# One ring of eight PSUM banks, and transposes of the new inverse instead of a second product in each level of the delta rule

## The chip, the cores and the metric

The kernel runs on one core of a Trainium2 chip. The metric is the device time of one execution in microseconds (us), as the median of several runs. TensorE (PE), VectorE (DVE), ScalarE (ACT), GpSimd (POOL) and SyncE (SP, which issues the DMAs) each run their own list of instructions and wait for one another on semaphores.

## The reference

One sequence of 512 tokens of width 1024, in fp32, goes through two blocks. The change touches the gated delta rule of the first block: 8 heads, keys and values of width 128, in chunks of 64 tokens. Cut to its core:

```python
h = rms_norm(x, norm1_w) * (1 + scale1) + shift1
proj = h @ w_in                                       # q, k, v, z, alpha, beta, attention, gates
qkv = silu(causal_dwconv(concat(dn_q, dn_k, dn_v), dn_conv_w))      # 4 taps over time
q, k = l2_norm(...), l2_norm(...)                     # per head
decay = exp(gc[:, None] - gc[None, :]) on the lower triangle       # gc = cumsum(g)
a_mat = strict_lower((k * beta) @ k.T * decay)        # 64 x 64 for each chunk and head
u, w = triangular_solve(I + a_mat, [v * beta, k * beta * exp(gc)])
intra = lower((q @ k.T) * decay)
# then the recurrence over 8 chunks: v_new = u - w S;  o = q_e S + intra v_new;  S = dec S + k_dec.T v_new
```

The rest of the first block is latent attention, output projections, a gated mix and a feed-forward part with a convolution. The second block has spatial gating, gated linear attention, band attention, a convolution of 31 taps, a gated merge and a feed-forward part.

## The kernel before

One function, `program(f)`, lists the stages; it is run once for each engine's class (`Tensor`, `Scalar`, `Vector`, `Gpsimd`), whose methods issue what that engine does. So the order of the calls is the order of each engine's queue. Stages that share time are generators, and `weave(main, side, n_main, n_side)` (L179) steps them: after each step of `main` it takes n_side / n_main steps of `side`. A point such as `dp_ve xt 2 h` is a semaphore value that the producer raises and others wait for.

**Linears.** A step of `main` is one unit: 128 output columns for all 512 tokens, made by 24 matmuls of 128x512 (three fp32r products, high x high, low x high, high x low, for each of 8 slices of the 1024 inputs) into one PSUM bank. The high halves of the weights (`whi`) are split off by ACT (L357), the low halves (`wlo`) by DVE or POOL (L360). A unit named dn0 to dn23 is a head's q, k or v; ACT and DVE then read its bank for the convolution, on DVE three `SCALAR_TENSOR_TENSOR` taps (L368), and ACT applies silu. Between them stand small matmuls of the modulation (`ada`), a few steps after certain units.

**Banks.** PSUM has eight banks, each 128 x 512 fp32. A `Banks` object is a ring: `take` gives the next bank that isn't held, `free` is the point at which the last user of that bank has read it, and PE waits for that point before it writes. `PL` (L332) has banks 0 to 2 for the units, `PA` (L333) has banks 3 to 7 for all other products of the program.

**The delta rule's side work** is `prep(h, w)`, four pairs of heads one after the other, the two heads of a pair stepped in turn. Its products each fill one bank with four 128x128 blocks (two chunks of 64 in each). A head's steps on PE: the sums of squares for k and q (`sq`); the decay row (`g`); `kk` and `qk` and the beta row (`b`); a transpose of k (`kt`); a transpose of the first inverse Xt (`x`); then levels 1 to 5; then `v` (a transpose), `w` and `u`. The stretch from `sq` to the first product of level 1 is called the preamble here, the rest the levels. ACT takes ln and exp of the norms, copies evacuated blocks, and DVE scales k and q, forms the decay differences (L365), and multiplies the masks in.

A level doubles the blocks of which the inverse is known. Xm holds the inverse, Xt its transpose, Bm the part of A of this level (made by POOL, `bm`), Dm the evacuated product. Level lv makes t = Bm' Xm (ACT copies it to Dm), then Xm -= Xt' Dm (`xm`) and Xt -= Dm' Xt (`xt`), the two subtractions on DVE from PSUM. Level 5 updates Xt alone. In the trace a fp32 matmul of 128x128 shows as two rows and a transpose (L345) as one.

**Order.** The units ahead of the stage are the first four of `qkv`; the rest of them, with the small projections behind them, run against the four pairs' side work, 21 rounds to a pair, 3.33 to a unit (30 : 100, the numbers of `weave`). SP's list of weight loads is written by the same stages and follows the buffers.

## Time and profile before

| | |
|---|---|
| median of 3 runs | 2551.38 us (2550.47 to 2552.47) |
| profiled execution | 2550.77 us |
| its span on the core | 2548.8 us |
| PE busy | 2361.8 us (93%), 10928 rows |
| DVE busy | 1090.6 us (43%), 1588 rows |
| ACT busy | 926.9 us (36%), 1352 rows |
| POOL busy | 699.7 us (27%), 415 rows |
| chain that ended last | PE 76%, DVE 11%, ACT 7% |
| mean granted clock of PE | 0.961 |

The span is the profiler's time from the first to the last instruction; the execution's own time is 2.0 us longer. The chain that ended last is followed back from the last instruction, and its shares tell on which engine the end rests. A busy share is the time in which an engine had an instruction in work; matmuls overlap, and the end of each is modelled.

### The profile page before, as it was taken

The page shows a single profiled execution, that of the slowest core. Times are in us where ns is not written, and L with a number is a line of the kernel's source. Part 1 is how long each engine was busy: PE and PEld are TensorE (multiplying, and loading weights), DVE is VectorE, ACT ScalarE, POOL GpSimd, SP SyncE. Part 2 cuts the span into 40 slices and gives each one's busy share as a digit, 9 for nine tenths or more (in the row PEclk, how much of TensorE's full clock was granted, in tenths as well). Part 3 has the DMA queues.
Part 4 walks back from the last instruction along what each step waited for, and adds up shares of the span by engine and source line. Part 5 has one row for each costly group of instructions (what it writes and reads, how often), then busy time and mean ns, then how long its engine had stood idle before and what let it go on. Part 6 is the DMA issues. An engine that isn't in the chain of part 4 may idle for free.

```text
span 2548.8 us, 27018 instructions
## 1 busy us (share of the span) xinstructions
PE 2361.8 (93%) x10928; PEld 1883.4 (74%) x10928; DVE 1090.6 (43%) x1588; ACT 926.9 (36%) x1352; POOL 699.7 (27%) x415
## 2 busy tenths in 40 slices
PE   8798989999899999899999887999999999999996
PEld 4577877986567677688888676787777777888875
DVE  2576656455443432433321599413443242322333
ACT  2544423233433432533322332334552433332334
POOL 1141144001211235222223241321132353332332
PEclk9898989999999899999999898999999999999998
DMA  8222223121122133333333421332221332333341
GB/s 263 75 67 68 73 59 100 50 75 54 38 66 70 42 99 95 117 95 96 95 99 99 124 75 58 92 99 66 83 67 58 108 91 76 107 92 98 100 123 50
DMA packets 347983, 220.65 MB, mean 87 GB/s; under 512 B 18393, under 2 KB 327244, under 8 KB 347860
## 3 DMA queue, kind: packets, MB, share of 16 engines
q1 hardware_dynamic: 338462, 202.31, 27.3%
q10 hardware_dynamic: 9398, 16.62, 2.0%
q8 instruction: 87, 1.43, 0.2%
q14 instruction: 36, 0.29, 0.0%
HBM read 210.49 MB, written 8.41 MB: 86 GB/s over the span
## 4 chain that ended last, share of the span: by engine, by line
PE 76%; DVE 11%; ACT 7%; issue 3%; POOL 2%; DMA 1%; ACTq 0%; SPq 0%; DVEq 0%; POOLq 0%
PE ps L342 74%; DVE arena L368 4%; ACT arena L357 3%; DVE arena L360 2%; DVE scr L368 1%; PE ps L345 1%; POOL wlo L360 1%; ACT whi L357 1%; ACT scr L357 1%; ACT L353 1%; POOL arena L360 1%; DVE wlo L360 1%; DVE arena L365 1%; DVE scr L360 0%; POOL scr L360 0%
## 5 line engine op out<-in xcount | busy, mean ns | idle before, releaser
L342 PE MATMUL ps<-hhi,whi 128*128 128x512 f32 x1664 | 676.6, 407 | 53.3 <-POOL wlo L360 32.3
L360 POOL TENSOR_TENSOR wlo<-wraw,whi 128x1024 fp32r<-128x1024 f32 (+1 forms) x163 | 389.7, 2391 | 1204.7 <-ACT whi L357 1204.7
L342 PE MATMUL ps<-hlo,whi 128*128 128x512 f32 x1664 | 661.5, 398 | 0.0
L342 PE MATMUL ps<-hhi,wlo 128*128 128x512 f32 x1664 | 660.7, 397 | 0.0
L357 ACT ACTIVATE whi<-wraw 128x1024 fp32r<-128x1024 f32 (+1 forms) x328 | 340.7, 1040 | 359.7 <-PE ps L342 298.1
L342 PEld LDWEIGHTS ps<-hhi,whi 128*128 128x128 f32 x1664 | 322.0, 194 | 134.7 <-issue 47.6
L342 PE MATMUL ps<-arena 128*128 128x128 f32 (+6 forms) x2304 | 341.6, 301 | 34.7 <-ACT arena L357 12.9
L360 DVE TENSOR_TENSOR wlo<-wraw,whi 128x1024 fp32r<-128x1024 f32 (+2 forms) x165 | 213.8, 1296 | 369.2 <-ACT whi L357 369.0
L342 PEld LDWEIGHTS ps<-hhi,wlo 128*128 128x128 f32 x1664 | 320.3, 192 | 69.4
L342 PEld LDWEIGHTS ps<-hlo,whi 128*128 128x128 f32 x1664 | 321.3, 193 | 68.0 <-issue 3.2
L342 PEld LDWEIGHTS ps<-arena 128*128 128x128 f32 (+1 forms) x2304 | 286.7, 197 | 70.0 <-issue 28.3
L357 ACT ACTIVATE arena<-ps 128x512 f32<-128x512 f32 (+5 forms) x223 | 116.4, 540 | 332.1 <-PE ps L342 277.1
L342 PE MATMUL ps<-h,whi 128*128 128x512 f32 x512 | 159.9, 394 | 1.1 <-POOL wlo L360 1.1
L357 ACT ACTIVATE scr<-ps,colv 128x512 f32<-128x512 f32 x78 | 55.4, 711 | 246.2 <-PE ps L342 241.1
L368 DVE SCALAR_TENSOR_TENSOR scr<-ps,colv,scr 128x511 f32<-128x511 f32 (+2 forms) x116 | 86.8, 749 | 132.6 <-ACT scr L357 130.2
L368 DVE SCALAR_TENSOR_TENSOR arena<-arena,colv 128x512 f32<-128x512 f32 (+1 forms) x136 | 132.0, 975 | 16.3 <-ACT arena L357 12.6
L360 DVE TENSOR_TENSOR arena<-ps,arena 128x512 f32<-128x512 f32 (+1 forms) x88 | 55.6, 640 | 153.3 <-PE ps L342 151.4
L360 DVE TENSOR_TENSOR scr<-ps,scr 128x512 f32<-128x512 f32 x86 | 59.1, 689 | 138.6 <-PE ps L342 137.0
L360 POOL TENSOR_TENSOR arena<-arena,scr 128x512 f32<-128x512 f32 x57 | 77.8, 1368 | 138.4 <-ACT scr L357 96.8
L342 PEld LDWEIGHTS ps<-h,whi 128*128 128x128 f32 x512 | 97.1, 190 | 22.6 <-issue 2.6
L342 PE MATMUL ps<-ff,whi 128*128 128x512 f32 x352 | 108.4, 389 | 0.0
L360 POOL TENSOR_TENSOR arena<-arena,cst 128x512 f32<-128x512 f32 (+1 forms) x48 | 62.2, 1309 | 144.3 <-PE ps L342 76.7
(190 smaller groups left out, 2691.9 us busy)
## 6 DMA issues: line engine op xcount, KB each, us to landing
wraw<-in_w_in_dram SPq DMA_DIRECT2D x99, 512.0 KB, 3.9
wraw<-in_w_ff_dram SPq DMA_DIRECT2D x64, 512.0 KB, 4.0
wraw<-in_ffn_w_up_dram SPq DMA_DIRECT2D x44, 512.0 KB, 3.9
wraw<-in_w_ada_dram SPq DMA_DIRECT2D x32, 512.0 KB, 3.9
wraw<-in_w_gate_dram SPq DMA_DIRECT2D x32, 512.0 KB, 3.9
arena<-in_w_ada_dram SPq DMA_DIRECT2D x8, 1024.0 KB, 11.5
wraw<-in_ffn_w_down_dram SPq DMA_DIRECT2D x16, 512.0 KB, 3.9
wraw<-in_w_branch_dram SPq DMA_DIRECT2D x16, 512.0 KB, 3.4
```

The lines of the kernel that those rows point to most:

```text
L342: return pe.e.matmul(o, l, r, start=start, stop=stop)
L345: return pe.e.transpose(o, i, CST[0:n, C_ID:C_ID + n])
L353: ac.e.preload_act_table_set("natural_log_exp_and_others")
L357: return ac.e.activation(o, i, f, bias=bias, scale=scale, **kw)
L360: return q.e.tensor_tensor(o, a, b, op)
L365: return q.e.tensor_scalar(o, a, s1, s2, op0, op1)
L368: return ve.e.scalar_tensor_tensor(out=o, in0=a, scalar=s, in1=b, op0=op0, op1=op1)
```

## The change

Three edits. First, the two rings become one of eight banks, for the units and everything else. Second, in levels 1 to 4 the product `xm` and its subtraction on DVE go. In their place PE transposes the updated Xt (`turn_xt`, four transposes into one bank), which waits for DVE's subtraction `xt`, and ACT copies the bank to Xm (`copy_x`); t of the next level waits for that copy. A level then has three steps (t, xt, x) instead of two. Third, the numbers of `weave` go from 30 : 100 to 30 : 120, four side steps to a unit instead of 3.33; the side work of a pair has 25 rounds after and 21 before.

```diff
--- before.py
+++ after.py
@@ -329,8 +329,7 @@
         SG = Signals(lambda name: ctx.enter_context(nc.semaphore(name)), values)
         inc, at, last = SG.inc, SG.at, SG.last
         pe, ve, ac, po, sp = (Engine() for _ in range(5))
-        PL = Banks(SG, PS[0:3], places)
-        PA = Banks(SG, PS[3:8], places)
+        PL = PA = Banks(SG, PS, places)
         SCR = [SCRT[:, i, :] for i in range(NSC)]
         ident = CST[:, C_ID:C_ID + P]
         ones = CST[:, C_ONE:C_ONE + P]
@@ -836,7 +835,7 @@
             for _ in range(4):
                 next(first)
             f.token_cols()
-            weave(chain(first, paced(f.small_proj(), more)), f.prep_pairs(), 30, 100)
+            weave(chain(first, paced(f.small_proj(), more)), f.prep_pairs(), 30, 120)
             f.rec_start()
             weave(paced(f.mla_proj(), more), f.recur(), 8, 16)
             run(more)
@@ -1133,6 +1132,16 @@
                 EG, Dm, Am, Xm, Xt, Bm = (A[:, 36 + 6 * w + i, :] for i in range(6))
                 q, k, v = A[:, QB + h, :], A[:, KB + h, :], A[:, VB + h, :]
                 blk = [slice(b * P, (b + 1) * P) for b in range(4)]
+
+                def turn_xt(lv):
+                    bk = PA.take("dn", h, "x", lv)
+                    pe.wait_ge(*PA.free("dn", h, "x", lv))
+                    pe.wait_ge(*at("dp_ve", "xt", lv, h))
+                    for s in blk:
+                        t = tr(bk[:, s], Xt[:, s])
+                    t.then_inc(*inc("dp_mm", "x", lv, h))
+                    PA.put(("dn", h, "x", lv), "dp_act", "x", lv, h)
+
                 while 16 + h not in self.have:
                     yield
                 yield
@@ -1179,33 +1188,18 @@
                 t.then_inc(*inc("dp_mm", "kt", h))
                 PA.put(("dn", h, "kt"), "dp_ve", "kb", h)
                 yield
-                bk = PA.take("dn", h, "x")
-                pe.wait_ge(*PA.free("dn", h, "x"))
-                pe.wait_ge(*at("dp_ve", "xt", 0, h))
-                for s in blk:
-                    t = tr(bk[:, s], Xt[:, s])
-                t.then_inc(*inc("dp_mm", "x", h))
-                PA.put(("dn", h, "x"), "dp_act", "x", h)
+                turn_xt(0)
                 yield
                 for lv in range(1, 6):
                     bk = PA.take("dn", h, "t", lv)
                     pe.wait_ge(*PA.free("dn", h, "t", lv))
                     pe.wait_ge(*at("dp_po", "bm", lv, h))
-                    pe.wait_ge(*at("dp_act", "x", h) if lv == 1 else at("dp_ve", "xm", lv - 1, h))
+                    pe.wait_ge(*at("dp_act", "x", lv - 1, h))
                     for s in blk:
                         t = mm(bk[:, s], Bm[:, s], Xm[:, s], True, True)
                     t.then_inc(*inc("dp_mm", "t", lv, h))
                     PA.put(("dn", h, "t", lv), "dp_act", "t", lv, h)
                     yield
-                    if lv < 5:
-                        bk = PA.take("dn", h, "xm", lv)
-                        pe.wait_ge(*PA.free("dn", h, "xm", lv))
-                        pe.wait_ge(*at("dp_act", "t", lv, h))
-                        pe.wait_ge(*at("dp_ve", "xt", lv - 1, h))
-                        for s in blk:
-                            t = mm(bk[:, s], Xt[:, s], Dm[:, s], True, True)
-                        t.then_inc(*inc("dp_mm", "xm", lv, h))
-                        PA.put(("dn", h, "xm", lv), "dp_ve", "xm", lv, h)
                     bk = PA.take("dn", h, "xt", lv)
                     pe.wait_ge(*PA.free("dn", h, "xt", lv))
                     pe.wait_ge(*at("dp_act", "t", lv, h))
@@ -1215,6 +1209,9 @@
                     t.then_inc(*inc("dp_mm", "xt", lv, h))
                     PA.put(("dn", h, "xt", lv), "dp_ve", "xt", lv, h)
                     yield
+                    if lv < 5:
+                        turn_xt(lv)
+                        yield
                 bk = PA.take("dn", h, "v")
                 pe.wait_ge(*PA.free("dn", h, "v"))
                 pe.wait_ge(*at("qkv", 16 + h))
@@ -1709,6 +1706,11 @@
             def prep(self, h, w):
                 EG, Dm, Am, Xm, Xt, Bm = (A[:, 36 + 6 * w + i, :] for i in range(6))
                 q, k, v = A[:, QB + h, :], A[:, KB + h, :], A[:, VB + h, :]
+
+                def copy_x(lv):
+                    ac.wait_ge(*at("dp_mm", "x", lv, h))
+                    act(Xm, PA.of("dn", h, "x", lv)[:, :], ACT.Copy).then_inc(*inc("dp_act", "x", lv, h))
+
                 while 16 + h not in self.have:
                     yield
                 if h < 2:
@@ -1736,8 +1738,7 @@
                 yield
                 yield
                 yield
-                ac.wait_ge(*at("dp_mm", "x", h))
-                act(Xm, PA.of("dn", h, "x")[:, :], ACT.Copy).then_inc(*inc("dp_act", "x", h))
+                copy_x(0)
                 yield
                 for lv in range(1, 6):
                     ac.wait_ge(*at("dp_mm", "t", lv, h))
@@ -1745,6 +1746,9 @@
                     act(Dm, PA.of("dn", h, "t", lv)[:, :], ACT.Copy).then_inc(*inc("dp_act", "t", lv, h))
                     yield
                     yield
+                    if lv < 5:
+                        copy_x(lv)
+                        yield
                 yield
                 ac.wait_ge(*at("dp_mm", "w", h))
                 act(k, PA.of("dn", h, "w")[:, :], ACT.Copy).then_inc(*inc("dp_act", "w", h))
@@ -2476,12 +2480,11 @@
                 yield
                 for lv in range(1, 6):
                     yield
-                    if lv < 5:
-                        ve.wait_ge(*at("dp_mm", "xm", lv, h))
-                        tt(ve, Xm, Xm, PA.of("dn", h, "xm", lv)[:, :], ALU.subtract).then_inc(*inc("dp_ve", "xm", lv, h))
                     ve.wait_ge(*at("dp_mm", "xt", lv, h))
                     tt(ve, Xt, Xt, PA.of("dn", h, "xt", lv)[:, :], ALU.subtract).then_inc(*inc("dp_ve", "xt", lv, h))
                     yield
+                    if lv < 5:
+                        yield
                 ve.wait_ge(*at("dp_mm", "v", h))
                 ve.wait_ge(*at("dp_po", "bm", 5, h))
                 tt(ve, b4(Am), b4(PA.of("dn", h, "v")[:, :]), per_tok(TB), ALU.mult).then_inc(*inc("dp_ve", "vb", h))
@@ -3065,6 +3068,8 @@
                         level(lv + 1)
                     yield
                     yield
+                    if lv < 5:
+                        yield
                 yield
                 yield
 
@@ -3325,7 +3330,7 @@
             sp.e, SG.engine = eng, "sp"
             sync_program()
 
-        return SG.points, {**PL.made, **PA.made}
+        return SG.points, PL.made
 
 
 # ---- launch: one core; inputs and outputs as the reference has them ----
```

On TensorE, the levels of the second pair of heads (levels 1 and 2), between the unit dn5 and the next one. `ps3` is bank 3, each row is a head's product or transpose. Before (t and xt, xm of two heads in turn, from the first level's xm on):

```order
L342 MATMUL ps3<-arena 128x128 x4
L342 MATMUL ps4<-arena 128x128 x4
L342 MATMUL ps5<-arena 128x128 x4
L342 MATMUL ps6<-arena 128x128 x4
L342 MATMUL ps7<-arena 128x128 x4
L342 MATMUL ps3<-arena 128x128 x4
L342 MATMUL ps4<-arena 128x128 x4
L342 MATMUL ps5<-arena 128x128 x4
L342 MATMUL ps6<-arena 128x128 x4
L342 MATMUL ps7<-arena 128x128 x4
```

After, at the same place in the program, behind dn5 (t and xt of level 2, then x, then t of level 3):

```order
L341 MATMUL ps7<-arena 128x128 x4
L341 MATMUL ps0<-arena 128x128 x4
L341 MATMUL ps1<-arena 128x128 x4
L341 MATMUL ps2<-arena 128x128 x4
L344 MATMUL ps3<-cst,arena 128x128 x4
L344 MATMUL ps4<-cst,arena 128x128 x4
L341 MATMUL ps5<-arena 128x128 x4
L341 MATMUL ps6<-arena 128x128 x4
```

Ten products became eight rows, of which two are transposes (L344, the old L345); in each level the transposes stand behind the xt that they read, with the other head's xt or x between, and the banks run through all eight.

On TensorE, the preamble of the third pair of heads (4 and 5). `gb,sel` are the decay and beta rows. Before, behind the unit dn22 and ahead of the products of the modulation:

```order
L342 MATMUL ps6<-arena 128x128 x4
L342 MATMUL ps7<-arena 128x128 x4
L342 MATMUL ps3<-gb,sel 128x512
L342 MATMUL ps4<-arena 128x128 x4
L342 MATMUL ps5<-arena 128x128 x4
L342 MATMUL ps6<-gb,sel 128x512
L345 MATMUL ps7<-cst,arena 128x128 x4
L345 MATMUL ps3<-cst,arena 128x128 x4
L345 MATMUL ps4<-cst,arena 128x128 x4
L345 MATMUL ps5<-cst,arena 128x128 x4
```

After, the same products stand ahead of dn22, behind `sq`:

```order
L341 MATMUL ps3<-gb,sel 128x512
L341 MATMUL ps4<-gb,sel 128x512
L341 MATMUL ps5<-arena 128x128 x4
L341 MATMUL ps6<-arena 128x128 x4
L341 MATMUL ps7<-gb,sel 128x512
L341 MATMUL ps0<-arena 128x128 x4
L341 MATMUL ps1<-arena 128x128 x4
L341 MATMUL ps2<-gb,sel 128x512
```

and behind dn22:

```order
L344 MATMUL ps4<-cst,arena 128x128 x4
L344 MATMUL ps5<-cst,arena 128x128 x4
L344 MATMUL ps6<-cst,arena 128x128 x4
L344 MATMUL ps7<-cst,arena 128x128 x4
L341 MATMUL ps0<-arena 128x128 x4
L341 MATMUL ps1<-arena 128x128 x4
L341 MATMUL ps2<-arena 128x128 x4
L341 MATMUL ps3<-arena 128x128 x4
```

kk and qk of both heads moved ahead of dn22; the transposes stay behind it, and now t of level 1 and its xt follow in the same place between the units.

## Rows read from the trace of the kernel before

**Rows 1.** The profile's page: span, and busy us of TensorE and VectorE.

```profile
span 2548.8 us, 27018 instructions
...
PE 2361.8 (93%) x10928; PEld 1883.4 (74%) x10928; DVE 1090.6 (43%) x1588; ACT 926.9 (36%) x1352; POOL 699.7 (27%) x415
```

**Rows 2.** Windows: us, busy us of PE, PEld, DVE, ACT, POOL (rows), PEclk, DMA share, GB/s.

```profile
121.40:467.60 346.20, 315.68 (x1898) 270.94 (x1897) 211.40 (x302) 135.34 (x203) 109.96 (x78) 0.94 0.25 71
```

**Rows 3.** The same view, sum over the four stretches of levels.

```profile
sum 195.10, PE 192.92 PEld 178.14 DVE 116.36 ACT 59.21 POOL 61.79; mean PE 48.23 PEld 44.54 DVE 29.09 ACT 14.80 POOL 15.45
```

**Rows 4.** The same view: preambles of the second, third and fourth pair.

```profile
217.10:247.00 29.90, 21.15 (x85) 15.01 (x84) 21.70 (x36) 13.97 (x20) 7.62 (x8) 0.81 0.22 68
306.80:344.30 37.50, 29.82 (x125) 23.03 (x124) 21.89 (x37) 15.41 (x22) 12.68 (x10) 0.77 0.19 57
398.40:423.50 25.10, 22.69 (x108) 16.56 (x108) 17.70 (x28) 13.77 (x21) 9.98 (x9) 1.00 0.24 70
```

**Rows 5.** TensorE's waits in the stage: us in total, times, longest us.

```profile
PE ps L345 <- DVE arena L360: 9.5, 6, 3.7
PE ps L342 <- DVE arena L365: 8.8, 6, 3.2
```

**Rows 6.** Timeline of TensorE: start us, us, line, op, count [idle before].

```profile
199.95 1.04 PE L345 MATMUL ps<-cst,arena 128*128 128x128 f32 x8
200.82 3.74 PE L342 MATMUL ps<-arena 128*128 128x128 f32 x32
```

**Rows 7.** Timeline of all engines around a unit and a level, second pair.

```profile
249.83 0.48 PE L342 MATMUL ps<-hhi,whi 128*128 128x512 f32 x1
...
255.38 3.73 PE L342 MATMUL ps<-arena 128*128 128x128 f32 x32
255.58 0.69 ACT L357 ACTIVATE scr<-ps,colv 128x512 f32<-128x512 f32 x1 [3.93 <-PE ps L342]
...
256.30 2.32 DVE L368 SCALAR_TENSOR_TENSOR scr<-ps,colv,scr 128x511 f32<-128x511 f32 x3 [3.21 <-ACT scr L357]
258.54 2.47 DVE L360 TENSOR_TENSOR arena<-arena,ps 128x512 f32<-128x512 f32 x4
...
259.36 3.67 PE L342 MATMUL ps<-arena 128*128 128x128 f32 x28 [0.25 <-DVE arena L360]
...
260.53 0.60 ACT L357 ACTIVATE arena<-ps 128x512 f32<-128x512 f32 x1 [3.74 <-PE ps L342]
```

**Rows 8.** Timeline of TensorE in the second pair's preamble.

```profile
226.89 1.16 PE L342 MATMUL ps<-arena 128*128 128x128 f32 x8 [1.95 <-DVE arena L365]
229.20 2.07 PE L342 MATMUL ps<-arena 128*128 128x128 f32 x8 [1.15 <-DVE arena L365]
...
231.93 0.79 PE L342 MATMUL ps<-hhi,whi 128*128 128x512 f32 x1
...
239.23 1.03 PE L345 MATMUL ps<-cst,arena 128*128 128x128 f32 x8
243.94 1.09 PE L345 MATMUL ps<-cst,arena 128*128 128x128 f32 x4 [3.67 <-DVE arena L360]
246.12 1.11 PE L345 MATMUL ps<-cst,arena 128*128 128x128 f32 x4 [1.09 <-DVE arena L360]
```

**Rows 9.** Windows, three microseconds of the unit at 231.93.

```profile
232.50:235.50 3.00, 3.00 (x8) 2.31 (x7) 2.97 (x4) 0.00 (x0) 3.00 (x5) 0.50 0.00 0
```

**Rows 10.** Timeline of TensorE at the start of the program.

```profile
9.79 5.74 PE L345 MATMUL ps<-cst,arena 128*128 128x128 f32 x33 [6.33 <-DMA arena<-in_x_dram]
```

**Rows 11.** Windows, two pieces of that run of transposes.

```profile
9.80:13.70 3.90, 3.90 (x19) 3.90 (x20) 2.30 (x4) 2.82 (x5) 0.00 (x0) 1.00 1.05 388
13.80:15.50 1.70, 1.70 (x17) 1.53 (x16) 1.70 (x4) 0.00 (x0) 0.00 (x0) 1.00 1.05 387
```

**Rows 12.** Timeline of TensorE ahead of the stage.

```profile
82.57 0.80 PE L342 MATMUL ps<-hhi,whi 128*128 128x512 f32 x1 [4.63 <-ACT arena L357]
...
100.78 0.77 PE L342 MATMUL ps<-hhi,whi 128*128 128x512 f32 x1 [5.69 <-POOL wlo L360]
```

## The prediction

> **What bounds the kernel now.** I read the page first. TensorE (PE) works for 2361.8 of 2548.8 us [rows 1], VectorE (DVE) and ScalarE (ACT) for less than half of it. So what counts is work taken from PE, and places where PE stands still. The edits touch one stage, from the first side work of the delta rule to the end of the fourth pair of heads, 346.2 us with 315.68 us of PE work [rows 2]. Windows cut it into two kinds of stretch. In the four stretches of levels (the doubling of the inverse, then v, w, u) PE is busy 192.92 of 195.10 us: a pure PE bound [rows 3]. In the four preambles (norms, kk, qk, decay, transposes, up to the first product of level 1) it stands still for 8.75, 7.7 and 2.4 us in the second, third and fourth (stretch less PE busy), with a granted clock of 0.81, 0.77 and 1.00 [rows 4]. The list of waits of the stage says who is waited for: its two costliest lines name DVE [rows 5]. So there are two prices, work in the levels and stalls in the preambles.
>
> **A. PE work in the levels.** Each head makes `xm` at levels 1 to 4: 8 x 4 = 32 products of four 128x128 matmuls. An fp32 matmul is two rows of the trace. 32 rows from 200.82 on show 3.74 us [rows 6]; some 0.2 us of it is the modelled tail of the last, so 0.112 us a row, and a head's four matmuls take 8 x 0.112 = 0.894 us. A transpose is one row: 8 rows from 199.95 to 200.82, 0.109 us each, and a head's four take 0.437 us [rows 6]. Replaced one for one: 32 x (0.894 - 0.437) = **-14.6 us**, sure at full clock. The 32 DVE subtractions that go (0.6 us each) and the 32 ACT copies that come (0.60 us, the row at 260.53 [rows 7]) move 19 us from one engine to the other; both have room, so neither is counted as such.
>
> **B. Handovers in the levels.** Before, `xm` and `xt` both need only the copy of t, and four products of two heads lie beside the evacuations. After, one level is the chain t, ACT copy, xt, DVE subtraction, transposes, ACT copy, t. PE has two heads to alternate, and now and then a projection unit (24 rows, 5.5 us, 249.83 to 255.38 [rows 7]). By the new order of TensorE I walked the 16 level-and-pair places:
> - No unit between xt and x, nine times. Four rows of the other head's xt (0.894 us) cover part of head 0's evacuation, which needs the product's tail, two semaphore steps and 0.6 us of DVE. What is left I take as 0.6: 5.4 us.
> - A unit with a convolution stands ahead of xt and x directly (in pair 0 and 1, and once in pair 2), three times. DVE must run the three taps first (256.30, 2.32 us, behind ACT's reading of the unit's bank) and subtracts from 258.54 on [rows 7]. The second xt ends by 1.79 us after the unit, x's input is there some 3.98 us after it: 2.2 us of wait, 2.65 with the second head. 8.0 us. Before, the same 3.98 us was covered by four products, leaving the 0.25 us at 259.36 [rows 7].
> - A unit ahead of x and then t, four times: ACT's copy for t stands behind what ACT does with the unit's bank (0.69 us at 255.58 and a second step like it [rows 7]); about 1.1 each, 4.5 us.
> - t to xt, as today, seven times 0.16: 1.1 us.
> Together 19.0 us, less what the same places cost today by starts of rows (0.2 to 0.4 beyond the pace; 259.36 less 255.38 is 3.98 where 32 rows need 3.58 [rows 7], some 13 of them, 5.4 us): **+13.6 us**. Bounds: 0, if the evacuations hide (two heads alternate), and +22, if every x costs like the middle kind for both heads. I take the walk. A and B nearly cancel.
>
> **C. Preambles.** The third edit gives 4 side steps per unit instead of 3.33, and the two orders shift what stands where; the ring changes which bank a product waits for.
> - Pair 1. Today PE stops 1.95 and 1.15 us for a bank that the DVE decay step frees, runs the unit of 231.93 in 7.3 us up to 239.23 against 5.5, and stops 3.67 and 1.09 us for the transposes' input [rows 8]. With the short waits ahead of kk that is 11.6 us. Now one unit stands between the squares and g (it hides the ln, exp and normalising chain) and the waits for banks go: with eight banks the one that kk takes was freed long before. What comes back: head 2's x still needs DVE's chain, and three taps, 2.32 us as at 256.30, stand ahead of it [rows 7]; 3.6 us, and 2 us of lower clock. **-6** (-7.4 to -5).
> - Pair 2. Its stretch is the longest, 37.5 us with 29.82 us of PE work at clock 0.77 [rows 4]: 7.7 us idle, and about 5 us of slow pace. The six products go ahead of a unit now, the transposes follow it, and level 1 starts at once. The ln chain is uncovered, about 4 us as today, and 1.6 us ahead of x: 12.7 - 5.6 = **-7** (-8.6 to -5).
> - Pair 0: two units lie in its chain of ACT and DVE today, one after: **+2.5** (0 to +4). Pair 3: busy 22.69 of 25.10 us at clock 1.00 today [rows 4]; here the unit that hid the ln chain moves behind it: **+1** (0 to +2.5).
> Sum **-9.5 us**, bounds -12 (each at its best) and 0 (the chain of DVE sets each preamble whatever PE does).
>
> **D. The clock in the levels.** Where PE stood still in the preamble the granted clock fell: 0.50 (1.2 GHz) for 232.50 to 235.50, three microseconds of the unit that stands behind two bank waits [rows 8, 9]. Such a fall costs that unit 1.9 us, 7.3 against 5.5 [rows 7, 8]. B puts waits of 2.2 us and less into the levels, with dense work between them; the two waits of pair 1 before the fall were 1.95 and 1.15 within 6 us [rows 8]. I take half a fall: **+1** (0 to +14, seven falls).
> Transposes alone seem to lift the clock: the program's first 33 rows are transposes after 6.33 us of idleness [rows 10], and the window at 9.80 has 19 rows in 3.90 us, the one at 13.80 17 in 1.70 us, 0.205 and 0.100 each [rows 11]. The clock column reads 1.00 in both, but the pace halves within one run of rows, from that of 1.2 GHz to that of 2.4, with no matmul between. The Trainium skill says otherwise (TensorE: Matmul & The Clock Gate, Part 4, PE-mode transpose): a transpose doesn't count as busy for the clock gate. By that sentence the 128 new transposes would be idle time and the fall of D would come in most levels, with the sum some 10 us nearer to no change; by the rows they keep the clock, and the sum stands. The trace disagrees with the page so far as pace tells it, and I go by the trace.
>
> **E. The ring elsewhere.** Outside the stage PE waits for a bank at few places. The longest, 4.63 us at 82.57, stands ahead of a stop of 5.69 us at 100.78 for weights that POOL splits, which takes up what is won [rows 12]; of smaller ones in the second block I take: **-1.5 us** (-4 to 0). If a projection unit met a bank whose reader is late, it would be a loss; with eight in turn each bank was put seven products earlier, and I see none.
>
> **Sum.** -14.6 + 13.6 - 9.5 + 1 - 1.5 = -11.0 us on the profiled execution's 2550.77 us: 2539.8. The median, 2551.38, stands 0.6 us above it: **2540.5 us**. 0.2% (5.1 us) is about what a measurement of this kernel can tell from no change.
>
> **The rivals.**
> - The preambles don't shorten (C = 0). For it: DVE is busy 21.70 of 29.90 us there [rows 4], so its chain may set the end whatever PE does; against: a bank wait is no data, and PE's stops are in both halves. A + B + D + E = -1.5: **2549.9 us**. No measurable change. Chance 0.20.
> - The handovers hide (B at half, +6). For it: PE has only 2.2 us of idleness in the four stretches today, two heads alternate, and ACT is busy for 59.21 of their 195.10 us, so its copy rarely stands in a queue [rows 3]. Then 2540.5 - 7.6 = **2533 us**. Chance 0.15.
> - Slower: the clock. The waits ahead of x and t fall in level after level; if each of the seven places behind a unit ended in a fall, every next unit would run as 231.93 did, with the level's products beside it, 2.4 us a place [rows 8]: +17 in place of D's +1, and the preambles' gain goes with the same falls: about **2557 us**. It decides from about four falls with C at half. Against: the fall in [rows 9] stands behind two waits close together with little between them, and B's have dense work between them. Chance 0.13, of which 0.03 is the case that transposes leave the clock down.
> - The forecast case, -6 to -16: the rest, 0.52.
>
> **How the numbers follow.** Likeliest 2540.5; its own range is 2535 to 2545. Faster: the forecast case and the hidden handovers, 0.67. Same: 0.20. Slower: 0.13. The range 2532 to 2551 takes in both neighbours and leaves out the slower case and the tail below: under 2 in 10.
>
> **What would show it.** In the profile after: 256 fewer matmul and 128 more transpose rows; in the levels some 15 to 20 us of new PE idleness, released by DVE and ACT lines of the kind in [rows 5], with starts of transposes 0.6 to 2.6 us late; level windows about as long as today; pair 1's and pair 2's preambles 5 to 8 us shorter and with a clock above 0.9; no wait of kk for the decay step. Wrong if the level windows shrink by more than 8 us (B too dear), if the preambles stay (C), or if the clock in the levels falls below 0.95 (D).

## The result, and the profile after

The changed kernel takes 2542.78 us (median of 6 runs, 2541.43 to 2545.0) against 2551.89 us (6 runs, 2550.17 to 2554.03) for the kernel before: ratio 0.9965, 95% interval 0.9953 to 0.9978, that is 9.1 us or 0.35% faster. The prediction was 2540.5 us, 11 us faster. The profiled execution is the slowest of the six, 2545.0 us, 2.2 us above their median, so its pieces are read to about 2 us.

The profile's page of the changed kernel, its span and the busy line of each engine:

```profile
span 2543.1 us, 26802 instructions
...
PE 2345.8 (92%) x10800; PEld 1867.6 (73%) x10800; DVE 1063.7 (42%) x1556; ACT 945.5 (37%) x1384; POOL 699.2 (27%) x415
```

Against [rows 1] PE has 128 rows fewer (256 of matmuls less, 128 of transposes more) and 16.0 us less work, DVE 26.9 us less, ACT 18.6 us more. The span fell by 5.7 us only; where, the windows tell. I cut the program at two instructions that both kernels have: the first `sq` of head 0, and the first product of the recurrence. First the kernel before, then the changed one; columns as in [rows 2].

```profile
124.70:473.10 348.40, 321.18 (x1920) 275.50 (x1921) 211.63 (x302) 133.65 (x201) 110.97 (x78) 0.94 0.24 69
473.10:2548.80 2075.70, 1944.36 (x8639) 1546.78 (x8637) 830.15 (x1211) 747.45 (x1088) 568.38 (x320) 0.97 0.29 85
```

```profile
126.40:477.20 350.80, 309.36 (x1793) 260.04 (x1793) 185.99 (x270) 152.08 (x233) 109.02 (x78) 0.95 0.25 69
477.20:2543.10 2065.90, 1939.86 (x8639) 1545.83 (x8637) 828.68 (x1211) 747.69 (x1088) 569.18 (x320) 0.97 0.29 85
```

This is the surprise. The stage that the prediction worked out didn't get 9.5 us shorter but 2.4 us longer in this execution: PE has 11.8 us less to do in it and stands still 14.2 us longer (27.2 to 41.4). What lies behind it, which the new products don't touch, got 9.8 us shorter. The missing 1.7 us stand ahead of the stage, where the PE rows are the same. Over the kernels of the table below the first `sq` starts between 123.7 and 127.4, and that goes with the program's first run of transposes, which begins at half pace and goes on at full pace, earlier or later by execution: 5.74 us in [rows 10] and, in the changed kernel,

```profile
9.76 6.60 PE L344 MATMUL ps<-cst,arena 128*128 128x128 f32 x33 [6.25 <-DMA arena<-in_x_dram]
```

It is 5.16 us in the two executions that start the stage at 123.7 and 123.8, and 6.5 to 6.8 us in all that start it behind 126. So this part is no doing of the edits; of those two executions one has two rings there and one has one.

In the stage, what replaced [rows 5] as PE's waits:

```profile
PE ps L344 <- DVE arena L359: 27.8, 19, 5.9
PE ps L341 <- ACT arena L356: 11.3, 9, 3.3
PE ps L344 <- DVE arena L364: 2.0, 2, 1.7
PE ps L344 <- DVE scr L367: 1.4, 1, 1.4
PE ps L341 <- DVE arena L359: 1.3, 4, 0.6
PE ps L341 <- DVE scr L367: 0.7, 1, 0.7
```

The waits for the decay step's bank (L365 before, L364 now: 8.8 us in six of [rows 5]) are 2.0 us. The transposes (L344) wait 27.8 us for DVE in 19 places where they waited 9.5 in six. The kinds of place of part B look like this on PE, in the first pair (units left out):

```profile
172.17 1.95 PE L341 MATMUL ps<-arena 128*128 128x128 f32 x16
176.06 1.25 PE L344 MATMUL ps<-cst,arena 128*128 128x128 f32 x8 [1.94 <-DVE arena L359]
177.49 3.93 PE L341 MATMUL ps<-arena 128*128 128x128 f32 x32 [0.18 <-ACT arena L356]
...
186.73 1.03 PE L344 MATMUL ps<-cst,arena 128*128 128x128 f32 x8
188.77 3.87 PE L341 MATMUL ps<-arena 128*128 128x128 f32 x32 [1.00 <-ACT arena L356]
192.53 0.66 PE L344 MATMUL ps<-cst,arena 128*128 128x128 f32 x4
193.51 0.63 PE L344 MATMUL ps<-cst,arena 128*128 128x128 f32 x4 [0.33 <-DVE arena L359]
```

and on DVE at the first of them:

```profile
173.09 2.32 DVE L367 SCALAR_TENSOR_TENSOR scr<-ps,colv,scr 128x511 f32<-128x511 f32 x3 [7.60 <-ACT scr L356]
175.32 1.27 DVE L359 TENSOR_TENSOR arena<-arena,ps 128x512 f32<-128x512 f32 x2
```

At 172.17 xt of both heads follows the unit; DVE's taps run to 175.4, the subtractions behind them, and x starts at 176.06. From the end of the 16 rows at their pace (1.79 us) to the start of x that is 2.1 us, where the prediction had 2.2 (again at 277.62 and 375.57). At 188.77 t waits for ACT's copy behind a unit, by 1.16 us over the pace, where I took 1.1. And 192.53 to 193.51 is the handover without a unit: 0.98 us for four rows that need 0.44, so 0.54, where I took 0.6.

The same view of the preambles and levels, cut where `sq` of the pair's first head and t of level 1 start. First the preambles of the four pairs:

```profile
126.40:159.40 33.00, 24.58 (x108) 18.23 (x109) 22.93 (x35) 15.58 (x23) 12.81 (x10) 0.84 0.20 52
217.00:245.10 28.10, 23.98 (x108) 17.66 (x108) 21.08 (x36) 19.20 (x27) 8.05 (x8) 0.94 0.13 38
310.70:332.00 21.30, 17.18 (x85) 12.09 (x84) 16.27 (x28) 13.98 (x20) 7.15 (x8) 1.00 0.09 26
397.70:422.40 24.70, 18.04 (x85) 12.82 (x84) 17.84 (x28) 11.37 (x17) 11.16 (x10) 0.92 0.28 74
```

then the levels:

```profile
159.40:207.70 48.30, 44.68 (x305) 39.70 (x305) 23.21 (x31) 19.75 (x32) 14.75 (x10) 1.00 0.28 85
245.10:305.20 60.10, 54.10 (x329) 48.09 (x329) 32.85 (x44) 21.08 (x34) 11.26 (x8) 0.91 0.30 88
332.00:392.10 60.10, 55.48 (x346) 48.74 (x345) 28.84 (x41) 21.43 (x34) 23.55 (x14) 0.94 0.33 84
422.40:471.60 49.20, 47.13 (x321) 42.70 (x320) 15.86 (x22) 17.53 (x28) 16.01 (x11) 0.97 0.21 60
```

The stretches hold other numbers of units than [rows 3, 4], so their lengths don't compare; PE's idleness and clock do. Pair 1's preamble (the second row) has 4.1 us of idleness instead of 8.75 and a clock of 0.94 instead of 0.81; pair 2's 4.1 instead of 7.7 at 1.00 instead of 0.77; pair 3's 6.7 instead of 2.4 at 0.92 instead of 1.00; pair 0's 8.4 instead of 5.0 at 0.84 as before. So the four preambles stand idle as long as before, 23.3 us against 23.9; what they gained is clock. The four stretches of levels have 3.6, 6.0, 4.6 and 2.1 us of idleness, 16.3 together, where the sum of [rows 3] has 2.2. And their clock, 1.00 or 0.98 before, is 0.91, 0.94 and 0.97 in three of them.

Idleness and clock can be put in one sum. At full clock a row keeps a pace from start to start: 0.227 us for one of 128x512 in a unit, 0.112 for an fp32 one of 128x128, 0.109 for a transpose. What a stretch takes beyond its rows at that pace is waits, the slow starts around them and slow clock. This is my working from the starts of the rows, to about 0.5 us:

| us beyond the pace | before | changed | no_ring (below) |
|---|---|---|---|
| preambles of pairs 0, 1, 2, 3 | 10.9, 14.4, 14.7, 4.1 | 12.1, 7.2, 5.8, 9.2 | 12.3, 10.4, 9.9, 9.3 |
| preambles together | 44.1 | 34.2 | 42.0 |
| levels together | 8.0 | 34.3 | 22.0 |
| of that, rows at 1.2 GHz | 1.1 | 9.0 | 0 |

The granted clock of the whole stage is 0.94 before and 0.95 after: the time at 1.2 GHz moved from the preambles into the levels.

### The profile page after: what moved, and what is told of

The parts are those of the page before. It is cut to its first block, busy times and chain, and to the rows that moved or that the text cites. A ratio compares the mean times of both kernels' runs of the same rounds, so it can differ in the third digit from the quotient of the medians.

```text
span 2543.1 us, 26802 instructions
## 1 busy us (share of the span) xinstructions
PE 2345.8 (92%) x10800; PEld 1867.6 (73%) x10800; DVE 1063.7 (42%) x1556; ACT 945.5 (37%) x1384; POOL 699.2 (27%) x415
## 4 chain that ended last, share of the span: by engine, by line
PE 76%; DVE 11%; ACT 7%; issue 3%; POOL 3%; DMA 1%; ACTq 0%; SPq 0%; DVEq 0%; POOLq 0%
PE ps L341 74%; DVE arena L367 4%; DVE arena L359 3%; ACT arena L356 3%; PE ps L344 2%; POOL wlo L359 1%; DVE scr L367 1%; ACT whi L356 1%; ACT scr L356 1%; ACT L352 1%; POOL arena L359 1%; DVE wlo L359 1%; DVE arena L364 1%; DVE scr L359 0%; ACT L356 0%
## 5 line engine op out<-in xcount | busy, mean ns | idle before, releaser
L341 PE MATMUL ps<-arena 128*128 128x128 f32 (+5 forms) x2048 | 313.3, 306 | 31.5 <-ACT arena L356 19.9
L341 PEld LDWEIGHTS ps<-arena 128*128 128x128 f32 (+1 forms) x2048 | 259.6, 198 | 65.1 <-issue 31.0
L356 ACT ACTIVATE arena<-ps 128x512 f32<-128x512 f32 (+5 forms) x255 | 135.2, 547 | 334.1 <-PE ps L341 242.3
L367 DVE SCALAR_TENSOR_TENSOR arena<-arena,colv 128x512 f32<-128x512 f32 (+1 forms) x136 | 128.8, 952 | 16.3 <-ACT arena L356 12.6
L344 PE MATMUL ps<-cst,arena 128*128 128x128 f32 (+1 forms) x470 | 76.4, 298 | 58.0 <-DVE arena L359 33.7
L344 PEld LDWEIGHTS ps<-cst,arena 128*128 128x128 f32 (+1 forms) x470 | 58.3, 152 | 74.5 <-DVE arena L359 34.8
```

The source lines that it names most:

```text
L341: return pe.e.matmul(o, l, r, start=start, stop=stop)
L344: return pe.e.transpose(o, i, CST[0:n, C_ID:C_ID + n])
L356: return ac.e.activation(o, i, f, bias=bias, scale=scale, **kw)
L367: return ve.e.scalar_tensor_tensor(out=o, in0=a, scalar=s, in1=b, op0=op0, op1=op1)
```

## The experiments

Three edits make eight kernels, so I ran all of them, then moved the ring and VectorE's order. "Stage" is from the first `sq` to the recurrence and "behind" from there to the end of the span, both in the run's profiled execution, which can lie some us off the median. The ratios are to the kernel before as timed beside each run.

| kernel | median us | ratio, 95% interval | stage us | behind us |
|---|---|---|---|---|
| before | 2551.89 | | 348.4 | 2075.7 |
| changed (ring, transposes, 30:120) | 2542.78 | 0.9953 to 0.9978 | 350.8 | 2065.9 |
| ring_alone | 2541.65 | 0.9950 to 0.9975 | 345.7 | 2071.5 |
| transposes_alone | 2557.86 | 1.0015 to 1.0032 | 355.3 | 2075.1 |
| pace_alone | 2561.78 | 1.0029 to 1.0053 | 358.7 | 2074.9 |
| ring_and_pace | 2554.42 | 0.9999 to 1.0016 | 357.9 | 2065.4 |
| no_ring (transposes, 30:120) | 2550.03 | 0.9984 to 1.0002 | 346.4 | 2076.9 |
| old_pace (ring, transposes) | 2539.55 | 0.9940 to 0.9965 | 344.9 | 2067.3 |
| ring_late | 2545.88 | 0.9965 to 0.9985 | 348.2 | 2068.8 |

### ring_alone: the first edit alone

```diff
-        PL = Banks(SG, PS[0:3], places)
-        PA = Banks(SG, PS[3:8], places)
+        PL = PA = Banks(SG, PS, places)
```

> The kernel before with the one ring of eight banks and nothing else. In the profile of the changed kernel the stage of the delta rule got 2.4 us longer, and what lies behind it 9.8 us shorter. Theory 1 (the gain is the ring's, and lies outside the stage): 2538 to 2543 us, and the part behind the stage 8 to 10 us shorter than before. Theory 2 (the prediction's: the gain comes from transposes and preambles, the ring gives 1.5 us outside): 2545 to 2550 us.

2541.65 us, 10.1 us faster than the kernel before (2551.72 in these runs): as fast as the whole change. Theory 2, the prediction's, gave it 2545 to 2550 and fails. Of the two parts of theory 1 the total holds; the part behind is 4.2 us shorter in this execution, not 8 to 10, and the stage 2.7. But this execution, 2546.48 us, is the slowest of the run's five, 4.8 us above their median.

In its stage the waits for the decay step's bank are 0.6 us instead of 8.8, but transposes wait 20.1 us for DVE's input in 8 places instead of 9.5 in six. PE's idleness in the four preambles is 23 us as before: where the wait for a bank goes, the wait for DVE's input right behind it grows. In pair 1 it was 1.95 and 1.15 us for the bank and 3.67 and 1.09 for the input [rows 8]; in ring_alone it is 6.44 and 1.10 us for the input, at 241.76 and 243.95.

The last column of the table is firmer than any row of it. With two rings the part behind takes 2074.9 to 2076.9 us in four executions, with one ring 2065.4 to 2071.5 in five, so the ring is worth 3.4 us or more there whatever the other edits are, 7.9 us between the two means. PE's idleness in it is 130.0 to 131.3 us with two rings and 125.8 to 128.1 with one.

### no_ring: the two other edits

The changed kernel with the two old rings.

> The changed kernel with the two old rings (three banks for the units, five for the rest): the transposes and 30 : 120 alone. Theory 1: 2550 to 2555 us, no gain or a small loss. Theory 2: 2541 to 2545 us.

2550.03 us, interval 0.9984 to 1.0002: no change that can be told. The transposes and the pace were to bring the stage's 9.5 us, with some help of the ring in the preambles; without it they bring 1.7 by the medians, 4 at most by the interval. Where it went, its four stretches of levels show:

```profile
160.10:208.30 48.20, 44.51 (x306) 39.65 (x305) 23.32 (x31) 19.77 (x32) 14.76 (x10) 1.00 0.28 86
249.00:302.50 53.50, 49.87 (x329) 44.21 (x329) 28.67 (x40) 21.10 (x34) 10.06 (x8) 1.00 0.32 96
333.50:389.40 55.90, 52.15 (x345) 45.99 (x345) 25.22 (x36) 21.05 (x34) 19.57 (x12) 1.00 0.32 84
419.80:467.60 47.80, 45.82 (x320) 41.40 (x321) 16.76 (x22) 17.30 (x28) 16.42 (x11) 1.00 0.21 59
```

The clock is full in all four, and PE stands idle 13.1 us where it did 2.2. By the table above the levels cost 14.0 us more beyond the pace, where part B had 13.6, and the stage's rows at their pace need some 15 us less, as in part A. But the preambles cost only 2.1 us less: with two rings they didn't shorten, and PE's waits for the decay step's bank are 9.5 us there, 8.8 in [rows 5].

### ring_and_pace, old_pace

The changed kernel with one edit undone: `xm` as before, and `f.prep_pairs(), 30, 100)`.

> The kernel before with the one ring and 30 : 120, the product xm kept. Tells what the transposes are worth where ring and pace are as in the changed kernel (2542.8 us). Theory 1: the preambles gain by ring and pace and the levels keep their cover, so 2534 to 2540 us: the transposes cost more than they save. Theory 2 (transposes replace 14.6 us of work by 13.6 us of waits): 2543 to 2545 us.

> The changed kernel with 30 : 100 instead of 30 : 120. With 25 rounds for a pair the side work needs 30 units and the weave has some 26, so the last pair's levels lie bare. Theory 1 and 2 both: the uncovered levels cost 10 to 20 us, 2550 to 2560 us; if the levels with more units between them wait less by as much, 2543.

ring_and_pace is 2554.42 us: 12.8 us slower than the ring alone. Both theories were wrong here. old_pace is 2539.55 us, 12.2 us faster than the kernel before and the fastest of the study (3.2 us below the changed kernel; the two intervals overlap between 0.9953 and 0.9965, so that it is better than the changed kernel isn't shown). My expectation of 10 to 20 us of loss in uncovered levels was wrong too: the uncovered levels of the last pair hand over at 0.6 us a level like the others without a unit. So with the ring the pace of 120 doesn't help the transposes.

### pace_alone, transposes_alone

The kernel before with 30:120, and the kernel before with the transposes at 30:100.

> The kernel before with 30 : 120 and nothing else. With the ring the same step cost 12.8 us (2541.7 to 2554.4) where the product xm is kept, since the side work runs ahead of the units that it needs (25.7 us of waits for ACT against 5.9). If that is the pace's own, it costs as much here: 2560 to 2566 us. If it is a meeting of ring and pace, 2550 to 2555.

> The kernel before with the transposes in the levels, two rings and 30 : 100. With one ring they gained 2.1 us at this pace (2541.7 to 2539.6). If their price doesn't hang on the ring: 2548 to 2551 us. If waits for the five banks take it: 2552 or more.

2561.78 and 2557.86 us, 9.9 and 6.0 us slower than the kernel before, where the two together (no_ring) cost nothing: the pace's cost is its own, not a meeting with the ring, and at 30:100 the transposes' price hangs on the ring (-2.1 us with it, +6.0 without). At 30:120 they are worth 11.6 us with the ring and 11.8 without. They come with a third round in each level, and no run has the transposes without that round, or the round without them. The timeline of PE in pace_alone, at the second pair's first steps:

```profile
206.72 1.98 PE L342 MATMUL ps<-arena,cst 128*128 128x512 f32 x4 [1.81 <-ACT arena L357]
223.03 3.75 PE L342 MATMUL ps<-arena,cst 128*128 128x512 f32 x4 [4.23 <-ACT arena L357]
```

The first row is `sq` of head 2, the second that of head 3, 16 us later. With four side steps to a unit and only 21 rounds to a pair the side work has caught up with the units: head 3's `sq` has to wait for the unit that makes its input, and the ACT steps behind it, 4.23 us with PE at a stop and then at half pace (3.75 us for four rows; 1.98 in the row above). It happens at 315.42 again, and at 407.85 with 2.60 us. In the stage PE waits 26.1 us for ACT there, against 6.4 before. With three steps to a level a pair has 25 rounds, more nearly what the pace uses up, and most of this goes: one edit makes the other bearable. In transposes_alone the two longest lines of PE's waits in the stage are

```profile
PE ps L345 <- DVE arena L360: 14.2, 14, 3.7
PE ps L342 <- DVE arena L365: 13.6, 8, 3.3
```

13.6 us for the decay step's bank, 8.8 in [rows 5]; with the eight banks (old_pace) these waits are 2.1 us. That the five banks of the side work are short is so shown; that it is all of the 6.0 us is not: the waits for ACT are 12.9 us, 6.4 before and 9.5 in old_pace.

### ring_late: the ring behind the stage alone

Two rings up to `rec_start`, one ring of eight from there on; `View` is a ring within the ring.

```diff
+        RING = Banks(SG, PS, places)
+        PL, PA = View(RING, 0, 3), View(RING, 3, 8)
...
             weave(chain(first, paced(f.small_proj(), more)), f.prep_pairs(), 30, 100)
+            RING.split = False
             f.rec_start()
```

> The kernel before, with two rings up to the recurrence of the delta rule and one ring of eight banks from there on. Theory 1 (the ring's gain lies behind the stage): 2542 to 2545 us, near to the ring alone (2541.7). Theory 2 (the ring gains in the preambles, by waits for banks that go): 2549 to 2551 us.

2545.88 us, 6.0 us faster than the kernel before, a little above the first theory's range and far from the second's. The stage is what it was (348.2 against 348.4 us), and the rest, in the same view as above:

```profile
471.90:2540.70 2068.80, 1942.23 (x8639) 1547.39 (x8637) 828.86 (x1211) 748.30 (x1088) 571.31 (x320) 0.97 0.29 85
```

6.9 us shorter than the 2075.70 of before: 4.8 us less idleness (131.3 to 126.6) and 2.1 us less PE busy time, with the same 8639 rows. It is tempting to call the second part clock. Here is one place that speaks for it, the kernel before and ring_late at the same instructions (some 5 us apart by then):

```profile
925.00:945.00 20.00, 17.69 (x72) 14.15 (x71) 8.06 (x7) 12.01 (x20) 8.79 (x5) 0.91 0.38 117
```

```profile
920.00:940.00 20.00, 17.69 (x79) 14.32 (x78) 8.71 (x8) 12.80 (x20) 8.81 (x5) 1.00 0.32 101
```

The same 17.69 us of PE work do 79 rows instead of 72, at clock 1.00 instead of 0.91. And one that speaks against it, before and ring_late again, at the same instructions:

```profile
1633.50:1638.50 5.00, 4.98 (x22) 4.16 (x23) 1.60 (x2) 2.01 (x2) 0.67 (x2) 1.00 0.38 111
```

```profile
1625.90:1630.90 5.00, 4.99 (x15) 4.00 (x16) 1.16 (x2) 1.88 (x2) 0.14 (x1) 0.66 0.37 111
```

Over the whole part the clock is no better, 0.97 in both; over the whole span it is 0.961 before and 0.959 here. So the gain isn't clock but waits. The busy time falls with them because the row before a wait is shown longer than its pace. The fall at 925 is in all the kernels with two rings and in none with one from there on, so it seems to be the ring's doing; other falls come in its place at other instructions. Of the single waits, the small ones went: 0.81 us at 805.23, 0.52 at 1571.57, 0.87 at 1583.62, 0.69 each at 1762.93, 1809.42 and 1851.70 of the kernel before, 4.3 us together. A long one moved on: the 4.01 us at 864.05 are gone, and the next product waits 4.53 at 862.33 instead.

### VectorE one step ahead

The waits of x at 176.06, 277.62 and 375.57 have the taps as their visible cause. `weave` got a start value, and VectorE's side work runs one step ahead of the units, so that the subtractions stand ahead of the taps:

```diff
-def weave(main, side, n_main, n_side):
+def weave(main, side, n_main, n_side, acc=0.0):
...
-            weave(chain(first, paced(f.small_proj(), more)), f.prep_pairs(), 30, 120)
+            weave(chain(first, paced(f.small_proj(), more)), f.prep_pairs(), 30, 120,
+                  1.0 if isinstance(f, Vector) else 0.0)
```

The first try, dve_first, took one step of the side work ahead of the weave itself, when head 1's input was not there yet; so head 0 alone was ahead.

> The changed kernel; VectorE alone takes its side work one round earlier, so that the subtraction that a transpose waits for stands ahead of the three taps of the unit. In the changed kernel x waits 2.2 us at 176.06, 277.62 and 375.57, 3.1 us at 251.86 and 5.4 us at 419.33. If the taps are the cause: 5 to 10 us faster than the changed kernel, 2533 to 2538 us. If the taps then come too late for ACT and the next pair: 2543 us or more.

> The changed kernel; VectorE alone is one step of side work ahead of the units, now for both heads of a pair (in the run before this one the second head's subtraction stayed behind the taps and x waited 3.8 us at 181.33). The waits of x behind taps at 176.06, 277.62 and 375.57 (2.2 us each) should go. If the taps were their cause and nothing takes their place: 6 to 8 us faster than the changed kernel, 2535 to 2537 us. If the delayed taps cost as much elsewhere (kk then stands ahead of the taps of dn10): 2542 us or more.

dve_first is 2551.94 us, 9.2 us slower than the changed kernel. The second head's subtraction still stood behind the taps (x waits 3.49 us at 181.33), so nothing was to be won; why it lost 9 us stays open. Its twelve runs lie between 2543.13 and 2556.19, and of the 7.6 us that the profiled one is longer 4.6 stand behind the stage, where the queues are those of the changed kernel. dve_first_both is 2544.44 us (ratio to the kernel before 0.9962 to 0.9985), no better than the changed kernel. Its profile says why. The longest waits in the stage:

```profile
PE ps L340 <- DVE scr L366: 16.1, 4, 7.4
PE ps L340 <- ACT arena L355: 13.5, 8, 3.3
PE ps L343 <- DVE arena L358: 8.8, 16, 2.6
PE ps L343 <- DVE scr L366: 6.1, 1, 6.1
```

Transposes wait 8.8 us for DVE's subtractions instead of 27.8: the cause was named rightly. But waits for DVE's taps (`scr`, L366) are 22.2 us instead of 2.1, two of them in PE's timeline:

```profile
145.64 1.11 PE L343 MATMUL ps<-cst,arena 128*128 128x128 f32 x4 [6.08 <-DVE scr L366]
...
234.14 0.79 PE L340 MATMUL ps<-gb,sel 40*128 40x512 f32 x1 [7.20 <-DVE scr L366]
```

Neither product reads anything of the taps. The row at 145.64 is `kt` of head 1, which takes the bank in which the unit dn10 lies; the taps are its last reader, and the wait is 4.7 us longer than in the changed kernel. The row at 234.14 is the beta row of head 3, on the bank of dn12. This is the price of one ring: a small product can stand behind a unit's evacuation, which it never could with two. In the changed kernel it costs 1.4 and 0.7 us (the two lines with `scr` above), at two places where the prediction's part E saw none.

The other three variants of it, at the old pace and with ScalarE ahead too:

> The changed kernel with 30 : 100 and VectorE one step ahead. At this pace (2539.6 us) only two x wait behind taps, 2.2 us each, so 2535 to 2537 us if it works; if VectorE's lead costs in the preambles, 2540 us or more.

> The changed kernel with VectorE and ScalarE both one step ahead of the units. The copies of x and t then stand ahead of ScalarE's reading of the unit's bank, so the waits of t behind a unit (1.27 us at 188.77, 291.62, 348.32, 1.6 at 445.95) should go too: 2 to 5 us less than VectorE alone ahead. If the units' convolution comes too late by it: more.

> The changed kernel with 30 : 100 and VectorE and ScalarE one step ahead. At this pace t waits 1.27 us behind a unit at three levels of the first pair (164.69, 175.91, 187.15) and x 2.2 us at two of the second: 2533 to 2536 us if all of it goes, 2540 or more if the preambles pay for it.

2552.76, 2579.89 and 2584.08 us: 13.2, 37 and 45 us slower than the same kernels without a lead. At the old pace VectorE's lead costs the same kind of waits in two preambles (6.60 us at 147.42 and 6.07 at 345.17, each ahead of a `gb,sel` row and released by the taps). With ScalarE ahead, by the order of its queue, the unit's bank is read only after the copies of a step that PE hasn't yet computed, and the taps wait for ScalarE; x of pair 0 waits 3.34 us at level 1 in dve_act_first where it waited next to nothing in the changed kernel. The order that was there, unit first on both engines, is the better one.

## Why the prediction was right, and where it wasn't

The number was right: 2542.78 against 2540.5, inside 2532 to 2551. It was luck in part: the sum came out near by two errors of opposite sign, the stage worse than forecast and the ring elsewhere better. "Beyond the pace" is the table's sum above.

- **A**, -14.6 us: the rows are as counted (128 fewer), the pace of a transpose is 0.11 us and the stage's rows at their pace need some 15 us less. Right.
- **B**, +13.6: right by its kinds, each measured to about 0.1 us (2.66, 1.16 and 0.54 us a place for 2.65, 1.1 and 0.6), and right in sum without the ring (14.0 us in no_ring). In the changed kernel the levels at full clock cost some 18 us more beyond the pace (7 to 25), 5 more than forecast. What the walk missed are places where an engine is late for other reasons: 2.79 us at 251.86, where DVE had still the masks of `kb` and the taps of dn20 ahead, and 0.72 us at 336.12, where xt waits for the taps of dn22 to give up a bank.
- **C**, -9.5: right in sum, -9.9 beyond the pace. Pairs 1 and 2 gained 7.2 and 8.9 us (-6 and -7 taken) and pair 0 lost 1.2 (+2.5 taken). Pair 3 lost 5.1 where I took 1, above its range: x of head 6 waits 5.09 us at 419.33, because DVE runs the whole chain from the decay step to the second inverse (405.91 to 419.2) and one unit doesn't cover it. Nearly all of the sum is clock and the slow starts around waits, as the idleness stayed at 23 us. It also needed the ring, which the text named only as one help of several: no_ring gained 2.1 us. Not in the sum is the 1.81 us that `sq` of head 2 waits at 216.97 for its input, the same starvation as in pace_alone.
- **D**, +1: the step that failed in the stage, too small by 7 us. The clock falls did come: windows on them in the changed kernel,

```profile
255.00:258.00 3.00, 3.00 (x9) 2.33 (x8) 1.23 (x1) 0.38 (x1) 0.00 (x0) 0.52 0.47 160
279.20:282.30 3.10, 3.10 (x18) 3.10 (x18) 0.00 (x0) 1.19 (x2) 1.11 (x1) 0.59 0.00 0
339.50:342.50 3.00, 3.00 (x9) 2.34 (x8) 0.23 (x2) 0.00 (x0) 2.04 (x1) 0.55 0.00 0
377.20:380.40 3.20, 3.20 (x17) 3.20 (x17) 0.00 (x0) 0.85 (x2) 0.00 (x0) 0.52 0.00 0
```

  four falls to 1.2 GHz in the levels of pairs 1 and 2, where the kernel before had only the tail of one from pair 1's preamble; the tail of a fifth, behind the 5.09 us of 419.33, reaches into pair 3's. Two of the four stand right behind the predicted waits of 2.2 us (277.62, 375.57), one at the 2.79 us of 251.86, the fourth behind several shorter ones. The units dn5 and dn7 take 7.6 and 7.2 us instead of 5.5; with the slow products it is 9.0 us, against 1.1 before. The third wait of 2.2 us (176.06) brought no fall, and no_ring, with three such waits, has none in its levels. That is the slower rival's mechanism, but at two of its seven places behind a unit (277.62, 375.57) and at two others; it didn't decide, because the preambles had less time at 1.2 GHz by as much as the levels had more, and the ring paid. The prediction's own sign against D, a clock below 0.95 in the levels, came true in two of the four.
- **E**, -1.5: the term that was mis-sized, and the one that made the result. Measured -6.9 us behind the stage by ring_late (-6.0 by medians, -3.8 to -8.9 by its interval), and -9.8 in the changed kernel's execution. The long wait that I took as worth nothing was one ahead of the stage (4.63 us at 82.57), and the one at 864.05 bears the argument out; but the small waits behind the stage are worth 4.3 us by themselves, where I took 1.5 for all.

So the stage, forecast at -9.5, measured +2.4 in one execution of the changed kernel. By medians the changed kernel is 2.6 us below ring_late by their ratios, with overlapping intervals, and the two have the same ring behind the stage; so the stage is worth a few us at most. For no_ring the rival "the preambles don't shorten" was the right forecast, with its mechanism: A and B came as summed, and of C 2.1 us. In the changed kernel the preambles did shorten, by C's 9.9 us, and the levels gave it back, 5 us by waits that the walk missed and 7 by the clock.

Two places of the prediction's working don't hold by themselves. Its slower rival says that the preambles' gain goes too, but 2557 us has only D's 16 us more in it; with C's 9.5 it would be 2566. And part E's "I see none" was wrong: with one ring a product did meet a unit's bank whose reader was late, for 1.4 and 0.7 us.

Why two edits that each cost 6 and 10 us cost nothing together is shown in part: most of the starvation of pace_alone goes (26.1 us of waits for ACT there, 15.3 in no_ring). Whether that is all of the 17.7 us is open, since the order of all units changes with it. Also open is why ring_alone gains 4 us in the stage by medians while the ring added to no_ring gains 1 there.

What the runs showed that nobody asked for: at 30:100 the ring and the transposes give 2539.55 us, the lowest median measured.

## What to carry to other kernels

Where one kernel has two rings of buffers, first try one ring by itself: here it was worth 10 us, as much as with the rewritten algorithm on top, and nothing of the computation changed. Its price is that a small product can wait for a big tile's last reader, so keep those readers prompt; whoever moves an engine's order must ask which bank it now frees late. An edit that replaces work by a longer chain of handovers is paid in waits (14 us for 15 us of work here), and paid twice where the granted clock falls behind them (9 us in the changed kernel): put both in the sum. To call a gain clock, take the granted clock over the whole stretch, not at the places where it rose. And a number that comes out right proves no step: the eight kernels of three edits showed that two of them together gained nothing.

## What was unexpected of the hardware

A clock fall followed single waits of PE within otherwise dense work, but not each of them. The wait of x behind the taps, shown as 1.94 us idle each time, comes ten times in four kernels: at 176.06, 277.62 and 375.57 of the changed one, at 176.67, 276.25 and 374.35 of no_ring, at 279.52 and 292.18 of old_pace, at 290.62 and 303.28 of transposes_alone. Behind 277.62, 375.57 and 292.18 the clock fell to 1.2 GHz; behind the other seven it stayed at 2.4. What decides is not shown.

Transposes alone went with a rising clock in the changed kernel too: in the line of 33 above they start some 0.21 us apart up to 15.5 and 0.11 apart behind it, with no matmul between, the same step of pace as in [rows 11]. The Trainium skill says that a transpose doesn't count as busy for the clock gate (TensorE: Matmul & The Clock Gate, Part 4, PE-mode transpose). These rows speak against it, and so does no_ring, which has the 128 new transposes and a clock of 1.00 in all four stretches of levels. Whether a transpose counts for less than a matmul right behind a wait, no run here separates.
